# Feed-forward pair 1 by the seven-product scheme, with its input forms made within pair 0

## The reference

```
def _swiglu(x, w_in, w_out):
    a, b = jnp.split(x @ w_in, 2, axis=-1)
    return (jax.nn.silu(a) * b) @ w_out
...
n = _modulate(_rmsnorm_2(h, norm_g[l, 0]), mod[:, 0, 0], mod[:, 0, 1])
h = h + 0.5 * mod[:, 0, 2] * _swiglu(n, ffn_w_in[l, 0], ffn_w_out[l, 0])
```

## Time and profile before

| | us |
|---|---|
| median of 3 runs | 3290.82 |
| profiled execution | 3291.03 |
| its span | 3289.2 |
| TensorE busy in the span | 3242.2 |
| VectorE busy | 2057.6 |
| ScalarE busy | 1461.0 |

### The profile page before, as it was taken

One profiled execution on the slowest core, in us unless ns is written; L12 is line 12 of the kernel. 1 busy time (PEld: TensorE's weight loads), 2 busy tenths in 40 slices (PEclk: granted clock), 3 DMA queues, 4 the chain that ended last, 5 costly groups with the idle time before them and its releaser, 6 DMA issues.

```text
span 3289.2 us, 52037 instructions
## 1 busy us (share of the span) xinstructions
PE 3242.2 (99%) x22014; PEld 2741.7 (83%) x22014; DVE 2057.6 (63%) x3459; ACT 1461.0 (44%) x2496; POOL 213.5 (6%) x319
## 2 busy tenths in 40 slices
PE   8999999999999999999999999999999999999998
PEld 6878767888888888888778899989998877789997
DVE  6675764678666665665654665666565666466655
ACT  5233565335344422234553444454444455344443
POOL 1000000101000010100000011101010000001110
PEclk9999999999999999999999999999999999999999
DMA  4010102655544365643112366736675321227764
GB/s 152 27 61 31 39 27 96 219 193 185 184 147 147 110 242 192 240 158 108 57 46 88 99 190 174 199 110 174 188 176 158 113 81 47 82 84 178 192 177 120
DMA packets 121193, 435.21 MB, mean 132 GB/s; under 512 B 13936, under 2 KB 16048, under 8 KB 120320
## 3 DMA queue, kind: packets, MB, share of 16 engines
q1 hardware_dynamic: 80928, 286.30, 24.8%
q0 software_dynamic: 40032, 145.58, 17.7%
HBM read 401.41 MB, written 2.10 MB: 123 GB/s over the span
## 4 chain that ended last, share of the span: by engine, by line
PE 91%; DVE 5%; ACT 2%; DMA 1%; issue 0%; POOL 0%; DVEq 0%; ACTq 0%; POOLq 0%
PE ps_run L479 90%; PE ps_run L871 1%; DVE wl L2246 1%; ACT nrm L1369 1%; ACT wh L1369 1%; DMA st<-wst 0%; DVE nrm L2246 0%; DVE X L2253 0%; PE ps_run L1219 0%; DVE HL L2253 0%; DVE nrm L2253 0%; DVE msk L2250 0%; DMA st<-st 0%; ACT HH L1369 0%; ACT bias L1369 0%
## 5 line engine op out<-in xcount | busy, mean ns | idle before, releaser
L2246 DVE TENSOR_TENSOR wl<-st,wh 128x1024 fp32r<-128x1024 f32 (+1 forms) x592 | 721.2, 1219 | 596.2 <-ACT wh L1369 594.3
L479 PE MATMUL ps_run<-HH,wh 128*128 128x512 f32 (+1 forms) x2560 | 911.2, 356 | 11.3 <-DVE HL L2253 3.2
L479 PE MATMUL ps_run<-HH,wl 128*128 128x512 f32 (+1 forms) x2560 | 893.4, 349 | 0.0
L479 PE MATMUL ps_run<-HL,wh 128*128 128x512 f32 (+1 forms) x2560 | 891.3, 349 | 0.0
L1369 ACT ACTIVATE wh<-st 128x1024 fp32r<-128x1024 f32 (+1 forms) x592 | 619.8, 1049 | 586.6 <-PE ps_run L479 453.0
L479 PEld LDWEIGHTS ps_run<-HH,wh 128*128 128x128 f32 x2560 | 485.0, 189 | 82.9 <-DVE HL L2253 6.0
L479 PEld LDWEIGHTS ps_run<-HL,wh 128*128 128x128 f32 x2560 | 485.2, 190 | 63.2 <-issue 3.8
L479 PEld LDWEIGHTS ps_run<-HH,wl 128*128 128x128 f32 x2560 | 484.8, 189 | 63.0
L479 PE MATMUL ps_run<-AH,wh 128*128 128x512 f32 (+1 forms) x1152 | 444.5, 386 | 1.2 <-DVE AL L2246 1.2
L479 PE MATMUL ps_run<-AL,wh 128*128 128x512 f32 (+1 forms) x1152 | 438.3, 381 | 0.0
L479 PE MATMUL ps_run<-AH,wl 128*128 128x512 f32 (+1 forms) x1152 | 438.1, 380 | 0.0
(11 more groups left out here) (453 smaller groups left out, 4026.6 us busy)
## 6 DMA issues: line engine op xcount, KB each, us to landing
st<-wst SPq DMA_DIRECT2D x538, 512.0 KB, 3.4
mb<-ada POOLq DMA_DIRECT2D x144, 512.0 KB, 4.8
st<-wst POOLq DMA_DIRECT2D x54, 512.0 KB, 7.4
st<-st POOLq DMA_DIRECT2D x54, 512.0 KB, 4.6
cw<-cw POOLq DMA_DIRECT2D x4, 1024.0 KB, 6.3
X<-xT SPq DMA_DIRECT2D x8, 256.0 KB, 6.3
X<-xT POOLq DMA_DIRECT2D x8, 256.0 KB, 4.2
out<-X SPq DMA_DIRECT2D x16, 128.0 KB, 1.8
```

What stands on the lines that cost most here:

```text
L479: i = self.e.matmul(out, lhsT, rhs, start=start, stop=stop, skip_group_check=True)
L2246: self.e.tensor_tensor(out, a, b, op).then_inc(*self.w.done(*points))
```

## The change

`FAST` begins with pair 1 instead of pair 2, so pair 1 goes by `fast_pair` in all three feed-forward parts that have pairs. The forms, which were made within pairs 0 and 1, are moved: on ScalarE all four high parts come within pair 0; on VectorE both portions and the low part of form 1 come within pair 0, those of forms 0, 2 and 3 in steps 0, 1 and 3 of pair 1. VectorE also waits for its own earlier instructions before it writes `c1` (`w.own()`), in every fast pair.

```
-FAST = tuple(range(2, 11))
+FAST = tuple(range(1, 11))
...
 (Act.plain_pair)
             self.finish_pair()
-            if g in (1, 2):
+            if g:
                 next(forms)
                 next(forms)
             finish(self.spend(8))
+            if g:
+                finish(forms)
             y = m.f[0 if g % 2 else 2]
...
 (Dve.fast_pair)
             if step == 2:
                 self.finish_pair()
-            if step == 3:
-                finish(forms)
+            if step in (0, 1, 3):
+                next(forms, None)
             for x, name in enumerate(("gate", "val")):
                 if step == 1:
+                    w.own()
                     summed(m.c1[x][:, part(0)], 0, x, name, "B", 1)
...
 (Dve.plain_pair)
             finish(self.spend(8))
-            if g < 4:
-                next(forms)
+            next(forms)
             y = m.f[0 if g % 2 else 2]
```

## The result

| | before | after |
|---|---|---|
| median, us | 3289.97 (3288.4 to 3292.22, 4 runs) | 3321.12 (3319.93 to 3321.9, 4 runs) |
| ratio, 95% interval | 1 | 1.0094 (1.0076 to 1.0111) |
| span of the profiled execution, us | 3289.2 | 3318.1 |
| matmuls | 22014 | 22230 |

The change makes the kernel slower by 0.94%, 31 us. 3319 us were forecast, in a range of 3305 to 3331.

What follows compares the result with a forecast made beforehand. TensorE's matmuls and its waits were taken to bound the kernel. Each part: -1.6 + 2.6 + 7.0 + 1.4 = +9.4 us, three parts +28.2 us, giving 3319 us; range 3305 to 3331.

Steps and rivals of the forecast that it cites:

- Saving: TensorE in pair 1: seven eighths of the columns save 1.6 us a part if TensorE never stands.
- First waits: Pair 1, steps 12 and s2: TensorE waits for a silu and a late split, 2.6 us a part.
- everything is worked out once and taken three times: Parts s10 and s11 were taken to repeat s01 instruction for instruction, so s01's sums were used three times.
- Second wait: Pair 2, step s2: TensorE stands 7.0 us a part for late transfers, bounds 4.2 to 13.
- the chain: Before pair 2's step s2: load 5.6 us, s1 to s2 7.3, s2 to landing 5.0, split 2.3.
- The clock: Behind the wait in pair 2, the clock falls to half rate, costing 1.4 us a part, bounds 0 and 2.8.
- rival 1: Clock stays up behind the wait: +8.0 us a part, 3315 us; chance 0.22.
- Rivals 2 to 4: Transfers in time, 3294 us (0.08); whole gain and no wait, 3286 us (0.03); waits spread, 3336 us (0.07).
- Rival 2: Pair 2's load, s1 and s2 take 3.8 us each and come in time: 3294 us; chance 0.08.
- The signs: Profile after: short waits in pair 1, ScalarE waiting some 10 us and TensorE about 7 in pair 2, clock below 1.00.

Runs made afterwards that it cites:

- e10: e8 with pair 2's four adding transfers left out, so part of the computation is missing: 3290.7 us (0.9999).
- e2: Changed kernel with ScalarE's silu of tile 1 ahead of the high parts of forms 2 and 3: 3316.78 us (1.0081).
- e8: e2's edit, plus VectorE's product of tile 1 before a form's low part, its AL in step s2 of pair 1, banks swapped in s10: 3312.76 us (1.0067).
- e1: Changed kernel with pair 2's four adding transfers left out in all three parts, so part of the computation is missing: 3298.13 us (1.0024).
- e4: Changed kernel with pair 2 plain, pairs 1 and 3 to 10 fast: 3303.42 us (1.004).
- e5: Changed kernel with pair 2's slabs loaded in the order r, r+2, r+3, r+1, r+4: 3308.29 us (1.0057).
- e7: Changed kernel with pair 2's loads in the order r, r+2, r+1, r+3, r+4 and its sum s3 issued behind s2: 3303.18 us (1.0039).
- e9: Changed kernel with the edits of e7 and e8 together: 3304.38 us (1.0041).
- e11: e9 with pair 2's last two slab loads held until its first adding transfer has landed: 3310.99 us (1.0062).

## Why the prediction was right

- **Saving, -1.6 a part: right.** A pair without waits takes 20.16 us after (2253.32 - 2238.92 for 120 matmuls, 14.40, and 5.76 for 48), and e10's starts close on it.
- **First waits, +2.6: right in mechanism and in size for s01** (2.8), the silu and the split where they were said to be: 1870.37 and 1874.57 with 1.24 and 1.09 us of idle time. In s11 the size is right (2.8) and half of the mechanism: both waits are for VectorE's splits, the first for that of slab 12, which the prediction had as 0.8 us late behind the forms. VectorE ended the split of s4 at 1881.1, the forecast 1882.0 less the 0.9 us by which s01 now begins earlier. Wrong for s10. The step "everything is worked out once and taken three times" failed, since the banks differ: +1.7 and a fall of the clock of 2.8, shown by e2 and e8.
- **Second wait, +7.0: right in mechanism, sized too large in two parts** (4.4, 4.9, 7.6; within 4.2 to 13). The mis-sized term is the chain: 4.6, 6.2 and 4.6 in s01 where 5.6, 7.3 and 5.0 were taken; in s11 the load alone was 7.0. (The load of pair 3 that the prediction calls alone had two others still under way, issued at 1900.60 and 1901.07.) e1 shows that without the transfers there is no wait, e4 that two fast pairs in a row are what it takes.
- **The clock, +1.4: too small by half, and its working was wrong.** It cost 2.8, 4.3 and 1.5, 8.6 in all. The prediction put the low clock of the stretch 10 to 20 us down to the wait of 8.0 us and said that a wait of 3.0 us "in mid-kernel" left no mark. The wait of 3.0 us is not in mid-kernel: it ends at 17.59 us, inside that very stretch. By stretches of 3 us, before (last three columns: PEclk, DMA share, GB/s):
```profile
9.00:12.00 3.00, 3.00 (x5) 1.09 (x4) 1.38 (x2) 2.52 (x5) 0.00 (x0) 1.00 1.06 415
...
15.00:18.00 3.00, 0.41 (x1) 0.41 (x2) 1.84 (x3) 2.04 (x4) 0.00 (x0) 0.85 1.07 426
18.00:21.00 3.00, 3.00 (x9) 2.33 (x9) 3.00 (x5) 1.66 (x3) 0.00 (x0) 0.58 0.81 328
```
 Behind the wait of 8.0 us, which ends at 8.00, the clock is full; behind that of 3.0 us it is low. So the rows taken for the price of a long wait were that of a short one, and the ground for rival 1 wasn't there. That 1.4 is near the 1.5 behind the second waits of s10 and s11 is luck. Rival 1 (the clock stays up) fell: it fell after every second wait, the shortest 4.3 us. And nothing was put down for a fall behind a first wait, which s10 had.
- **Rivals 2 to 4** did not occur. Rival 2 wanted three transfers of 3.8 us: measured were 4.6, 6.2 and 4.6. By the Trainium skill (DMA: Bandwidth & Descriptors, Anatomy of one DMA) a transfer of 512 KB takes 3.2 us, an estimate. SyncE's plain loads are near it (median 3.5 on the page after), the adding transfers are not (5.3 and 4.6 even alone). No wait arose in pair 3.
- **The signs** came, one of them smaller: ScalarE waited 6.7, 7.1 and 9.8 us for the adding transfer, where some 10 were said. The upper end of the range is 2 us above what 1.3 times waits and clock give (3329).
- So the sum was near in part by luck: errors ran against each other. The second waits were 4.2 us less than forecast, the clock 4.4 and the first waits 2.1 us more.

## What to carry to other kernels

Where a faster scheme shortens the steps of the engine that bounds, work out the deadline of every operand anew: here 1.6 us saved a pair moved deadlines by up to 5 us and left a chain of three transfers bare. A wait of TensorE may cost 1.4 to 2.8 us more in clock behind it, and not by its length: 2.8 behind 4.3 us, 1.5 behind 7.4. That loss is inside busy time, so read it from starts and from the granted clock by stretch, not from the sums, and place each wait in time before a stretch is read as its effect. Before copying one part's working to its twins, compare which bank or buffer each uses.

## What the hardware did that was not expected

- An adding transfer fills the DMA engines at less than half the rate of plain loads: alone it held 0.94 of them at 139 GB/s, while after 1884.00 in the changed kernel plain loads had 344 GB/s at a share of 0.87:
```profile
1884.00:1886.00 2.00, 2.00 (x19) 2.00 (x18) 1.48 (x2) 0.83 (x1) 0.00 (x0) 1.00 0.87 344
```
- Its company matters more than its source. Issues of the page after (KB each, median us to landing), from DRAM and from a slab in the on-chip memory:
```profile
st<-wst POOLq DMA_DIRECT2D x60, 512.0 KB, 7.5
st<-st POOLq DMA_DIRECT2D x60, 512.0 KB, 4.6
```
 Of the 60 from DRAM, 56 had another transfer beside them; the four that had none took 5.3 us. Alone, those from a slab take 4.6. So some 0.8 us of the 2.9 go with the source.
- The earlier s1 was issued, the longer it took to s2. Counted from the start of pair 1 in s01 it went out after 20.0 us in the changed kernel (6.2 to s2), 14.9 in e5 (8.8), 14.9 in e7 (8.75) and 14.4 in e9 (9.4). Loads beside it are part of it; e11, with one load, had 8.5. In these four slow ones a load went out within 0.2 us of s1, in the changed kernel the last was 2.7 us ahead. Whether that is the cause was not tried.
- The clock's answer to a wait is not told by the wait's length. It stayed up behind 1.84 us (e2, s10) and 2.75 us (e5, s01), fell to a mean of 0.57 over the next 4 us behind 1.94 us (e7, s01), and fell too behind 2.49 us (e9, s11) and 3.01 us (e5, s11). It isn't even told by the program: the wait of 3.0 us at the start is the same in every trace, and the stretch 18 to 21 us behind it has 0.58 before (above), but in e10 and in e1:
```profile
18.00:21.00 3.00, 2.54 (x12) 1.80 (x11) 3.00 (x5) 1.18 (x3) 0.00 (x0) 1.00 0.92 356
...
18.00:21.00 3.00, 3.00 (x9) 2.32 (x8) 3.00 (x5) 1.31 (x3) 0.00 (x0) 0.50 0.73 282
```
 The price of s10's first wait (4.1 us each time) varies too: 2.8 us after, 1.4 in e1, 1.6 in e4, 2.2 in e5. A difference of 1 to 3 us between two traces can be the clock alone. What tells the cases apart was not found.
